# mLSTM gate rows of heads 1 to 3 spread over the partitions by a transfer through memory

## The chip, the cores and the metric

The kernel runs on one core of a Trainium2 chip. The metric is the time on the device, in microseconds, of one execution of the whole program; the median of several runs is used.

## The reference

One inference step of a two-layer decoder for a prompt of 256 tokens and eight samples of four tokens (288 token columns in all). Layer 0 has a linear recurrence and a windowed attention, layer 1 an mLSTM block, each with an MLP. The part that matters is the mLSTM of layer 1, four heads of 512 columns, each with a 512 x 512 state:

```python
m_t = jnp.maximum(log_inter, jnp.max(log_intra, axis=2))
w_intra = jnp.exp(log_intra - m_t[:, :, None, :]) * jnp.einsum('bthd,bshd->btsh', qc, kc)
w_inter = jnp.exp(log_inter - m_t)
num = jnp.einsum('btsh,bshe->bthe', w_intra, vc) + w_inter[..., None] * jnp.einsum('bthd,bhde->bthe', qc, C)
den = jnp.sum(w_intra, axis=2) + w_inter * jnp.einsum('bthd,bhd->bth', qc, n)
h = num / jnp.maximum(jnp.abs(den), jnp.exp(-m_t))[..., None]
decay = jnp.exp(bcum[:, -1] + m - m_new)
C_new = decay[..., None, None] * C + jnp.einsum('bshd,bshe->bhde', kw, vc)
```

The quantities `m_t`, `exp(-m_t)`, `w_inter` and `decay` are one number per head and token (or per head and sample). The kernel holds them as rows, one partition a head, and needs them for each head on all 128 partitions.

## The kernel before

Every engine has its own instruction stream, written out by hand; the streams meet at semaphores. Dense projections run before (`IN_C`) and after (`OUT_C`) the head stage, as float32 products in three parts (lines 2140 to 2142).

**The rows.** During the last steps of `IN_C` VectorE and ScalarE compute `rows`, 4 partitions x 616 columns: minus the running maximum (256 prompt columns), the bound of the denominator (256), then for the samples the maximum, the weight of the old state and the decay. Of these 584 (`NBC`) are to be spread. ScalarE's exponentials (lines 1060 to 1062) finish them and count `gact` up to 3; TensorE's `gate_columns` waits for that.

**The spreading.** `head_rows(h)` on TensorE (line 2546) multiplies `rows` with a selection matrix of 4 x 128 (`sel`): a product of 512 columns and one of 72 (L2548, L2549). They land in the two staging banks, 6 and 7 of the eight PSUM banks, which each staged value of a head takes in turn. The list `USES` gives the order (q0 to q3, qo, kt0, kt1, ks, vt0, vt1, vs, bc0, bc1, sc, nu0, nu1, n, mean), `staged` waits until the value two places before has been read, and `reads` works out which count of which semaphore (`stage_read_a` for ScalarE, `stage_read_v` for VectorE) that is. ScalarE's `head_rows` copies both products to `bc` in SBUF (L1134, L1135); `bc` has two buffers, taken by even and odd heads.

**The readers of `bc`.** VectorE's `queries(h)` (L1783 and behind) scales the samples' queries and counts `qs_ready`; `arguments(h)` (L1798 to L1801) writes the arguments of the exponentials and counts `ew_arg`; the denominators take a row (L1892), and each state update `new_state` (L1831) a decay column.

**The order of a head.** A head has eight rounds j = 0 to 7. In each round TensorE multiplies two blocks of the old state with the samples' queries (`old_state`, L2615) and makes two outer products (`outers`, L2654), VectorE updates the two blocks in the ring `cring` (L1831), and SyncE stores them and loads the blocks eight places ahead (L666, L657). In rounds 3 and 4 TensorE also makes the prompt's state (L2640) and ScalarE copies it out (`prompt_state`, L1168, in its rounds 2 and 3). Each engine's `chunk(h, j)` puts the work of the next head between rounds:
- round 4: q (`qk`, L2495 and L2499; ScalarE L1072, L1074); round 5: keys; round 6: values (`vt0`, `vt1`, `vs`; ScalarE L1125 to L1130, VectorE L1776)
- round 7 on TensorE: `head_rows(h + 1)`, `sum_groups` (L2624), `scores(h + 1)` (L2558, L2561)
- round 7 on ScalarE: copy of the summed old states (L1211), `head_rows(h + 1)`, group sum (L1216), its square (L1218), the three exponentials `exps(h + 1)` (L1141 to L1143, with a table load), `own_values` (`vb`, L1153), `high_rows` (L1178, which releases GpSimd L2110)
- round 7 on VectorE: `queries`, `arguments`, `weights` (L1808, L1809) of head h + 1

For head 0 the same pieces stand before the loop: on TensorE `values_by_token(0)`, `head_rows(0)`, `scores(0)`; on ScalarE `own_keys(0)`, `values_by_token(0)`, `head_rows(0)`, `exps(0)`, `own_values(0, 0)`. `own_values` writes the right-hand side of the outer products, and `outers` waits for it (`vb_ready`).

Of the kernel before, what the change touches and what calls it, by code (L numbers as in the profile page):

```python
# [19 lines left out]
F32 = mybir.dt.float32  # L20
F32R = mybir.dt.float32r
ALU = mybir.AluOpType
ACT = mybir.ActivationFunctionType
AX = mybir.AxisListType

P = 128
D = 1024
SEQ = 256
NB = 8
# [21 lines left out]
NH = 4  # L51
# [25 lines left out]
IN_AB, OUT_AB, UP0, DOWN0, IN_C, OUT_C, UP1, DOWN1 = range(8)  # L77
# [11 lines left out]
OUT0 = [sum(m // P for _, m in DENSE[:i]) for i in range(8)]  # L89
# [16 lines left out]
NBC = R_DECAY + NB  # L106
# [14 lines left out]
assert ITEMS % 2 == 0  # L121

USES = ["q0", "q1", "q2", "q3", "qo", "kt0", "kt1", "ks", "vt0", "vt1", "vs",
        "bc0", "bc1", "sc", "nu0", "nu1", "n", "mean"]
VT_BANKS = (6, 7, 2, 3, 6, 7)
AB_USES = ["qs", "q0", "ks", "k0"] + [f"{g}{m}" for m in range(MT) for g in "ri"]
DVE_READS = ("ks", "vs", "sc", "nu0", "nu1", "n")
# [24 lines left out]
def program(nc, A, O):  # L152
    ctx = ExitStack()
    with ctx:
# [119 lines left out]
        sel, o = at("sel", o, NH * P, parts=NH)  # L274
# [15 lines left out]
        rows, o = at("rows", o, NROWS, parts=NH)  # L290
# [33 lines left out]
        bc, o = at("bc", rstd_at, 2, NBC)  # L324
# [15 lines left out]
        assert AT["conv_a_w"] + T <= AT["conv_c_w"]  # L340

        ps = ctx.enter_context(nc.psum_tensor("ps", [P, 8, 512], F32))

        def qz_of1(h, e, b):
            return qz1[:, h % 2, NS * (NB * e + b):NS * (NB * e + b) + NS]
# [24 lines left out]
        def sem(name):  # L370
            sems[name] = ctx.enter_context(nc.semaphore(name))
            return sems[name]
# [19 lines left out]
        out_taken = sem("out_taken")  # L392
# [3 lines left out]
        std_ready = sem("std_ready")  # L396
        rstd_ready = sem("rstd_ready")
        x_new = sem("x_new")
        xin_hi_ready = sem("xin_hi_ready")
        xin_ready = sem("xin_ready")  # L400
        relu2_ready = sem("relu2_ready")
# [57 lines left out]
        gact = sem("gact")  # L459
        gcol_ready = sem("gcol_ready")  # L460
# [4 lines left out]
        stage_full = sem("stage_full")  # L465
        stage_read_a = sem("stage_read_a")
# [10 lines left out]
        c_new = sem("c_new")  # L477
# [43 lines left out]
        def use(h, name):  # L521

            return len(USES) * h + USES.index(name)

        def reads(u):

            by_dve = USES[u % len(USES)] in DVE_READS
            n = sum(1 for j in range(u + 1) if (USES[j % len(USES)] in DVE_READS) == by_dve)
            return (stage_read_v if by_dve else stage_read_a), n
# [184 lines left out]
        def _(act):  # L714
# [349 lines left out]
            def staged(h, name):  # L1064
                u = use(h, name)
                act.wait_ge(stage_full, u + 1)
                return ps[:, 6 + u % 2]
# [36 lines left out]
                if g == G_PARTS + 8:  # L1104
                    keys_by_token(0)


            act.wait_ge(gcol_ready, 1)
            act.activation(tokg.rearrange("p a b -> p (a b)"), ps[:, 5, 0:4 * NH], ACT.Copy)
            act.activation(tokg_s.rearrange("p a b -> p (a b)"), ps[0:NS, 5, 4 * NH:6 * NH], ACT.Copy)  # L1110
# [11 lines left out]
            def values_by_token(h):  # L1122
# [6 lines left out]
                act.activation(vtk_s, src[0:NS], ACT.Copy)  # L1129
                act.activation(vst[:, h % 2], src, ACT.Copy, scale=sel3[:, 5:6]).then_inc(vst_hi_ready, 1)  # L1130

            def head_rows(h):

                act.activation(bc[:, h % 2, 0:512], staged(h, "bc0"), ACT.Copy).then_inc(stage_read_a, 1)  # L1134
                act.activation(bc[:, h % 2, 512:NBC], staged(h, "bc1")[:, 0:NBC - 512], ACT.Copy  # L1135
                               ).then_inc(stage_read_a, 1)

            def exps(h):

# [21 lines left out]
            def prompt_state(h, half):  # L1161

                i = item(h, NB, half)
                s = i % C_SLOTS
                act.wait_ge(c_mm, i + 1)
                if i >= C_SLOTS:
                    act.wait_ge(c_out[s], 16 * (i // C_SLOTS))
                act.activation(cring[s], ps[:, banks_of(i):banks_of(i) + HD2, :], ACT.Copy).then_inc(p_new, 1)  # L1168
# [11 lines left out]
            def chunk(h, b):  # L1180
                if b == 0:
                    act.wait_ge(den_psum, h + 1)
                    act.activation(stok[:, 0, h:h + 1], ps[0:NS, 3, SEQ:SEQ + 1], ACT.Abs)
                    act.activation(dn, ps[:, 3, 0:SEQ], ACT.Abs).then_inc(den_abs, 1)
                    act.activation(z[:, ET * h:ET * h + ET], z[:, ET * h:ET * h + ET], ACT.Silu).then_inc(z_ready, 1)
                if b == 1:
                    act.wait_ge(stage_read_v, reads(use(h, "nu1"))[1])
                    act.activation(qf[:, :, 0:SEQ], hT, ACT.Square).then_inc(h_sq, 1)
                if b == 2:
                    act.activation(dn, staged(h, "mean")[:, 0:SEQ], ACT.Sqrt, bias=tiny[:, 0:1], scale=1.0 / DH  # L1190
                                   ).then_inc(stage_read_a, 1)
                    if h == 2:
                        sample_roots(0)
                if b in (2, 3):
                    if h + 1 == NH:
                        act_hi(b - 2, 0, STEP0[OUT_C])
                    prompt_state(h, b - 2)
                if b == 4 and h + 1 < NH:
                    qk(h + 1)
                if b == 5 and h + 1 < NH:  # L1200
                    keys_by_token(h + 1)
                    own_keys(h + 1)
                if b == 6 and h + 1 < NH:
                    values_by_token(h + 1)
                    if h == 2:
                        sample_high(0)
                if b == 4 and h + 1 == NH:
                    high_rows(h)
                if b == 7:
                    act.wait_ge(hs_psum, h + 1)  # L1210
                    act.activation(hs4, ps[:, 2, :], ACT.Copy).then_inc(hs_copied, 1)  # L1211
                    if h + 1 < NH:
                        head_rows(h + 1)

                    act.wait_ge(hs_sum, h + 1)
                    act.activation(hs[:, h], ps[0:NS, 3, :], ACT.Copy).then_inc(hs_taken, 1)  # L1216
                    act.wait_ge(hs_taken, h + 1)
                    act.activation(hs_junk, hs[:, h], ACT.Square, accum_out=stok[:, 1, h:h + 1]).then_inc(hs_sq, 1)  # L1218
                    if h + 1 < NH:
                        exps(h + 1)  # L1220
                        own_values(h + 1, 0)
                        high_rows(h)

            act.wait_ge(out_taken, OUT0[OUT_C])
            own_keys(0)
            values_by_token(0)
            head_rows(0)
            exps(0)
            own_values(0, 0)
            for h in range(NH):  # L1230
# [19 lines left out]
        def _(dve):  # L1250
# [527 lines left out]

            def queries(h):

                dve.wait_ge(stage_read_a, reads(use(h, "bc1"))[1])
                inter = bc[:, h % 2, R_INTER:R_INTER + NS].unsqueeze(1).to_broadcast([P, ET, NS])
                order.after(dve.tensor_tensor(qn, qo, inter, ALU.mult))  # L1783
                if h == 0:
                    dve.wait_ge(qz1_zero, 1)
                for e in range(ET):
                    most, last = qz_own(h, e)
                    order.mark(dve.tensor_copy(most, seqs(qn[:, e, 0:NS - NT])))
                    order.mark(dve.tensor_copy(last, qn[:, e, NS - NT:NS]))
                order.wait()  # L1790
                n0_t = n0_of(h).unsqueeze(2).to_broadcast([P, ET * NB, NT])
                qn_t = qn.rearrange("p e (b t) -> p (e b) t", t=NT)
                dve.tensor_tensor(qn_t, qn_t, n0_t, ALU.mult).then_inc(qs_ready, 1)
# [333 lines left out]
        def _(pe):  # L2127
# [353 lines left out]
            def staged(h, name):  # L2481

                u = use(h, name)
                if u >= 2:
                    pe.wait_ge(*reads(u - 2))
                return ps[:, 6 + u % 2]
# [56 lines left out]
                    by_token(h, f"vt{tt}", 2, lambda m: xm[:, m, PAD + P * tt:PAD + P * tt + P])  # L2543
                samples_thrice(h, "vs", 2)

            def head_rows(h):
                hsel = sel[:, P * h:P * h + P]
                pe.matmul(staged(h, "bc0"), hsel, rows[:, 0:512], start=True, stop=True).then_inc(stage_full, 1)  # L2548
                pe.matmul(staged(h, "bc1")[:, 0:NBC - 512], hsel, rows[:, 512:NBC], start=True, stop=True  # L2549
                          ).then_inc(stage_full, 1)  # L2550

            def scores(h):

# [132 lines left out]
            def chunk(h, b):  # L2686
                if b == 0:
                    denominators(h)
                    pe.matmul(ps[0:NS, 2, :], ew[0:NS, 3 * P:3 * P + NS], vtk_s, start=False, stop=False,
                              skip_group_check=True)  # L2690
                    numerators(h)
                if h == 2 and b == 1:
                    sample_turns(0)
                if h == 2 and b == 4:
                    sample_scales(0)
                if h + 1 < NH:
                    if b == 4:
                        qk(h + 1)
                    if b == 5:
                        keys_by_token(h + 1)  # L2700
                    if b == 6:
                        values_by_token(h + 1)
                    if b == 7:
                        head_rows(h + 1)
                        sum_groups(h)
                        scores(h + 1)

            pe.wait_ge(gcol_taken, 1)
            values_by_token(0)
            head_rows(0)  # L2710
            scores(0)
            for h in range(NH):
                for j in range(NB):
# [165 lines left out]
```

## Time and profile before

| | |
|---|---|
| median of 3 runs | 1102.4 us (1102.11 to 1103.18) |
| profiled execution | 1102.52 us, span 1100.7 us |
| TensorE products | busy 1050.7 us, 95% of the span |
| VectorE | busy 664.3 us, 60% |
| ScalarE | busy 530.6 us, 48% |
| GpSimd | busy 188.8 us, 17% |
| chain that ended last | TensorE 79%, VectorE 10%, ScalarE 4% |
| head stage | about 632 to 833 us |
| spread products of heads 0 to 3 | from 636.7, 682.9, 731.2 and 779.9 us |

Busy times of engines overlap; TensorE's is modelled, and its products are pipelined, so that neighbouring rows overlap. In rows of the timeline the first number is the start in us from the span's start, the second the duration in us; brackets at the end hold the idle time of that engine before the row and what ended it. `PEld` is TensorE's weight load, `SPq` and `ACTq` are DMA issues in the instruction streams of SyncE and ScalarE.

### The profile page before, as it was taken

How to read it: one execution, taken by the hardware profiler on the slowest of the kernel's cores; microseconds unless marked ns; L12 is line 12 of the kernel's file. 1: busy time of each engine (PE TensorE's matmuls, PEld its weight loads, DVE VectorE, ACT ScalarE, POOL GpSimd, SP SyncE). 2: the span in 40 equal slices, each digit the busy share in tenths (PEclk: the TensorE clock that was granted, in tenths of full speed). 3: DMA queues.
4: the chain of work that ended last, by engine and by line, in shares of the span. 5: the costliest groups of instructions: out<-in, count | busy, mean ns of one | idle time of the engine just before them, and what ended most of it. 6: DMA issues, size and time to landing. Idle time of an engine off the chain costs nothing.

```text
span 1100.7 us, 21592 instructions
## 1 busy us (share of the span) xinstructions
PE 1050.7 (95%) x8473; PEld 912.0 (83%) x8473; DVE 664.3 (60%) x975; ACT 530.6 (48%) x865; POOL 188.8 (17%) x250
## 2 busy tenths in 40 slices
PE   6999999899999999999899999899989999999995
PEld 6988787688999999999899945363529999999995
DVE  5567694643485564335997566767784485564333
ACT  6333654533566553436565344462624466553431
POOL 5134000000114230101400420412100104230100
PEclk9999999999999999999999999999989999999998
DMA  9799887999545445454743069999998435454531
GB/s 349 261 349 337 315 339 282 381 376 409 177 135 171 159 168 171 159 167 137 273 152 118 1 212 406 351 400 349 375 402 322 160 134 172 164 162 171 166 120 43
DMA packets 92762, 261.23 MB, mean 237 GB/s; under 512 B 8933, under 2 KB 10085, under 8 KB 92409
## 3 DMA queue, kind: packets, MB, share of 16 engines
q1 hardware_dynamic: 91818, 258.69, 65.5%
q0 software_dynamic: 432, 1.29, 0.4%
q8 instruction: 55, 0.90, 0.3%
q14 instruction: 25, 0.20, 0.1%
q10 hardware_dynamic: 432, 0.14, 0.1%
HBM read 218.36 MB, written 41.73 MB: 236 GB/s over the span
## 4 chain that ended last, share of the span: by engine, by line
PE 79%; DVE 10%; ACT 4%; issue 2%; DMA 2%; POOL 2%; SPq 1%; DVEq 0%; ACTq 0%
PE ps L2140 20%; PE ps L2141 20%; PE ps L2142 20%; PE ps L2252 2%; PE ps L2654 1%; DVE cring L1831 1%; PE ps L2615 1%; PE ps L2640 1%; PE ps L2507 1%; PE ps L2333 1%; DVE w_lo L1256 1%; DMA kv_a<-in_kv 1%; PE ps L2234 1%; DVE x L1350 1%; PE ps L2495 1%
## 5 line engine op out<-in xcount | busy, mean ns | idle before, releaser
L1256 DVE TENSOR_TENSOR w_lo<-w_raw,w_hi 128x1024 fp32r<-128x1024 f32 x232 | 286.5, 1241 | 211.3 <-ACT w_hi L723 210.4
L723 ACT ACTIVATE w_hi<-w_raw 128x1024 fp32r<-128x1024 f32 x232 | 242.4, 1054 | 209.0 <-PE ps L2142 166.5
L2140 PE MATMUL ps<-xin_hi,w_hi 128*128 128x288 f32 x1016 | 304.9, 300 | 13.6 <-DVE w_lo L1256 13.6
L2141 PE MATMUL ps<-xin_lo,w_hi 128*128 128x288 f32 x1016 | 301.6, 297 | 0.0
L2142 PE MATMUL ps<-xin_hi,w_lo 128*128 128x288 f32 x1016 | 301.3, 297 | 0.0
L2140 PEld LDWEIGHTS ps<-xin_hi,w_hi 128*128 128x128 f32 x1016 | 192.8, 190 | 25.5 <-DVE w_lo L1256 15.1
L2141 PEld LDWEIGHTS ps<-xin_lo,w_hi 128*128 128x128 f32 x1016 | 192.9, 190 | 0.7
L2142 PEld LDWEIGHTS ps<-xin_hi,w_lo 128*128 128x128 f32 x1016 | 192.7, 190 | 0.0
L2141 PE MATMUL ps<-hid_lo,w_hi 128*128 128x288 f32 x512 | 151.0, 295 | 0.0
L2142 PE MATMUL ps<-hid_hi,w_lo 128*128 128x288 f32 x512 | 150.9, 295 | 0.0
L2140 PE MATMUL ps<-hid_hi,w_hi 128*128 128x288 f32 x512 | 150.2, 293 | 0.0
L2140 PEld LDWEIGHTS ps<-hid_hi,w_hi 128*128 128x128 f32 x512 | 96.3, 188 | 0.0
L2141 PEld LDWEIGHTS ps<-hid_lo,w_hi 128*128 128x128 f32 x512 | 96.3, 188 | 0.0
L2142 PEld LDWEIGHTS ps<-hid_hi,w_lo 128*128 128x128 f32 x512 | 96.2, 188 | 0.0
L1831 DVE SCALAR_TENSOR_TENSOR cring<-cring,bc,ps 128x1024 f32<-128x1024 f32 x64 | 79.0, 1276 | 26.8 <-PE ps L2654 26.5
L1995 POOL TENSOR_TENSOR hid_lo<-relu,hid_hi 128x288 f32 x64 | 61.6, 965 | 160.7 <-ACT hid_hi L805 160.7
L1371 DVE SCALAR_TENSOR_TENSOR relu<-ps,rstd 128x288 f32<-128x288 f32 x64 | 29.0, 456 | 62.0 <-PE ps L2142 56.2
L803 ACT ACTIVATE relu<-relu 128x288 f32<-128x288 f32 x64 | 28.2, 441 | 63.4 <-DVE relu L1371 58.7
L1985 POOL COPY sqsum<-sq 128x288 f32<-128x288 f32 x5 | 2.9, 570 | 296.8 <-ACT sq L791 289.4
L1988 POOL TENSOR_TENSOR sqsum<-sqsum,sq 128x288 f32<-128x288 f32 x31 | 25.0, 808 | 147.9 <-ACT sq L791 146.9
L791 ACT ACTIVATE sq<-ps 128x288 f32<-128x288 f32 x32 | 13.2, 412 | 69.5 <-PE ps L2142 69.5
L2654 PEld LDWEIGHTS ps<-vb,kst 64*128 64x128 f32 x128 | 13.0, 190 | 37.4 <-issue 20.3
(421 smaller groups left out, 1665.7 us busy)
## 6 DMA issues: line engine op xcount, KB each, us to landing
w_raw<-in_weights SPq DMA_DIRECT2D x232, 512.0 KB, 3.4
cring<-in_C SPq DMA_DIRECT2D x64, 512.0 KB, 6.4
out_Cs<-cring SPq DMA_DIRECT2D x64, 512.0 KB, 7.2
kv_a<-in_kv SPq DMA_DIRECT2D x56, 448.0 KB, 6.2
kv_b<-in_kv SPq DMA_DIRECT2D x52, 448.0 KB, 6.2
kv_w<-in_kv SPq DMA_DIRECT2D x20, 448.0 KB, 7.5
out_Cp<-cring SPq DMA_DIRECT2D x8, 512.0 KB, 6.7
out_v<-gaqkv SPq DMA_DIRECT2D x1, 1152.0 KB, 15.0
```

Of the source, the lines that this page charges most:

```text
L723: act.activation(w_hi[:, l % UM], w_raw[:, l % W_SLOTS], ACT.Copy).then_inc(hi_ready, 1)
L803: act.activation(relu2[:, l % 2], relu[:, l % 2], ACT.Square).then_inc(relu2_ready, 1)
L1256: dve.tensor_tensor(w_lo[:, l % W_SLOTS], w_raw[:, l % W_SLOTS], w_hi[:, l % UM], ALU.subtract).then_inc(lo_ready, 1)
L1371: dve.scalar_tensor_tensor(relu[:, l % 2], ps[:, bank, 0:T], 0.0, rstd, ALU.max, ALU.mult).then_inc(out_taken, 1)
L1831: dve.scalar_tensor_tensor(cring[s], cring[s], bc[:, h % 2, R_DECAY + b:R_DECAY + b + 1], new, ALU.mult, ALU.add).then_inc(c_new, 1)
L1988: pool.tensor_tensor(sqsum, sqsum, sq[:, m % 2], ALU.add).then_inc(sq_added, 1)
L1995: pool.tensor_tensor(hid_lo[:, bass.ds(m, 1)].rearrange("p a t -> p (a t)"), relu2[:, l], hid_hi[:, bass.ds(m, 1)].rearrange("p a t -> p ( ...
L2140: pe.matmul(out, w_hi[:, j, ws], hi, start=start and kk == 0, stop=False)
L2141: pe.matmul(out, w_hi[:, j, ws], lo, start=False, stop=False)
L2142: last = pe.matmul(out, w_lo[:, l % W_SLOTS, ws], hi, start=False, stop=stop and kk == UK - 1)
L2252: last = pe.matmul(ps[32 * b4:32 * b4 + 32, 4 + c, 0:NK // 2], qz_of[b4][:, h], kv[s][:, c * NK // 2:(c + 1) * NK // 2], start=h == 0, sto ...
L2654: last = pe.matmul(ps[:, banks_of(i) + d, :], kst[own, h % 2, P * e:P * e + P], vb[own, (HALF_B * h + p) % 2], start=True, stop=True)
```

## The change

The rows of all heads are stored once to an array in memory (`row_copy`), by a DMA from ScalarE's queue. For heads 1 to 3 a DMA from ScalarE's queue, issued in round 3 of the head before, reads one row and writes it to all 128 partitions of `bc`. The uses `bc0` and `bc1` go out of the list, so that `sc` follows `vs`. Head 0 keeps the products, in banks 3 and 2, with one count of `gcol_ready` behind both, and ScalarE copies them as `first_rows`. The ScalarE copies add 8 each to `bc_in` and the DMAs 16; VectorE's `queries` waits for that count.

```diff
 USES = ["q0", "q1", "q2", "q3", "qo", "kt0", "kt1", "ks", "vt0", "vt1", "vs",
-        "bc0", "bc1", "sc", "nu0", "nu1", "n", "mean"]
+        "sc", "nu0", "nu1", "n", "mean"]
...
+        row_copy = nc.dram_tensor("row_copy", [NH, NBC], F32).ap()
...
@@ ScalarE
+            act.wait_ge(gact, 3)
+            act.dma_start(row_copy, rows[:, 0:NBC]).then_inc(rows_out, 16)
             act.wait_ge(gcol_ready, 1)
...
+            def first_rows():
+
+                act.wait_ge(gcol_ready, 2)
+                act.activation(bc[:, 0, 0:512], ps[:, 3, :], ACT.Copy).then_inc(bc_in, 8)
+                act.activation(bc[:, 0, 512:NBC], ps[:, 2, 0:NBC - 512], ACT.Copy).then_inc(bc_in, 8)
+
             def head_rows(h):
 
-                act.activation(bc[:, h % 2, 0:512], staged(h, "bc0"), ACT.Copy).then_inc(stage_read_a, 1)
-                act.activation(bc[:, h % 2, 512:NBC], staged(h, "bc1")[:, 0:NBC - 512], ACT.Copy
-                               ).then_inc(stage_read_a, 1)
+                act.wait_ge(rows_out, 16)
+                if h >= 2:
+                    act.wait_ge(c_new, 2 * NB * (h - 1))
+                act.dma_start(bc[:, h % 2], row_copy[h:h + 1].to_broadcast([P, NBC])).then_inc(bc_in, 16)
...
                     prompt_state(h, b - 2)
+                if b == 3 and h + 1 < NH:
+                    head_rows(h + 1)
...
                     act.activation(hs4, ps[:, 2, :], ACT.Copy).then_inc(hs_copied, 1)
-                    if h + 1 < NH:
-                        head_rows(h + 1)
-
...
             values_by_token(0)
-            head_rows(0)
+            first_rows()
             exps(0)
...
@@ VectorE, queries
-                dve.wait_ge(stage_read_a, reads(use(h, "bc1"))[1])
+                dve.wait_ge(bc_in, 16 * (h + 1))
...
@@ TensorE
-            def head_rows(h):
-                hsel = sel[:, P * h:P * h + P]
-                pe.matmul(staged(h, "bc0"), hsel, rows[:, 0:512], start=True, stop=True).then_inc(stage_full, 1)
-                pe.matmul(staged(h, "bc1")[:, 0:NBC - 512], hsel, rows[:, 512:NBC], start=True, stop=True
-                          ).then_inc(stage_full, 1)
+            def first_rows():
+
+                hsel = sel[:, 0:P]
+                pe.wait_ge(out_taken, OUT0[OUT_C])
+                pe.matmul(ps[:, 3, :], hsel, rows[:, 0:512], start=True, stop=True)
+                pe.matmul(ps[:, 2, 0:NBC - 512], hsel, rows[:, 512:NBC], start=True, stop=True).then_inc(gcol_ready, 1)
...
                     if b == 7:
-                        head_rows(h + 1)
                         sum_groups(h)
                         scores(h + 1)
...
             values_by_token(0)
-            head_rows(0)
+            first_rows()
             scores(0)
```

ScalarE from the prompt state of head 0 to the q of head 1, before (line numbers in rows of the change are its own, some 3 to 11 higher):

```order
L1168 ACTIVATE cring_164<-ps 128x1024
L1168 ACTIVATE cring_167<-ps 128x1024
L1153 ACTIVATE vb<-vst,sel_119 128x512
L1072 ACTIVATE qf<-ps 128x288 x4
L1074 ACTIVATE qo<-ps 128x128
```

And in the change:

```order
L1179 ACTIVATE cring_164<-ps 128x1024
L1179 ACTIVATE cring_167<-ps 128x1024
L1147 DMA bc<-row_copy 128x584
L1164 ACTIVATE vb<-vst,sel_119 128x512
L1075 ACTIVATE qf<-ps 128x288 x4
L1077 ACTIVATE qo<-ps 128x128
```

The load of the next head's rows stands between the second prompt state and `vb`; nothing else moved there.

ScalarE at the start of head 1 (`hs_110` is `hs4`, the summed old states), before:

```order
L1130 ACTIVATE vst<-ps,sel_119 128x512
L1211 ACTIVATE hs_110<-ps 128x512
L1134 ACTIVATE bc<-ps 128x512
L1135 ACTIVATE bc<-ps 128x72
L1216 ACTIVATE hs<-ps 32x512
L1218 ACTIVATE hs_junk,stok<-hs 32x512
L1141 ACT_TABLE_LOAD
L1141 ACTIVATE ew<-ew,tokg 128x256
```

And in the change:

```order
L1134 ACTIVATE vst<-ps,sel_119 128x512
L1224 ACTIVATE hs_110<-ps 128x512
L1226 ACTIVATE hs<-ps 32x512
L1228 ACTIVATE hs_junk,stok<-hs 32x512
L1152 ACT_TABLE_LOAD
L1152 ACTIVATE ew<-ew,tokg 128x256
```

The two copies to `bc` are gone; the rest keeps its order.

TensorE at the same place, before:

```order
L2654 MATMUL ps<-vb,kst 128x512 x4
L2548 MATMUL ps<-rows,sel 128x512
L2549 MATMUL ps<-rows,sel 128x72
L2624 MATMUL ps<-hs_110,four_eyes 32x512
L2558 MATMUL ps<-qf,xcc 128x256 x4
L2558 MATMUL ps<-qf,xcc 128x128 x4
L2561 MATMUL ps<-qf,xcc 32x32 x4
```

And in the change:

```order
L2665 MATMUL ps<-vb,kst 128x512 x4
L2635 MATMUL ps<-hs_110,four_eyes 32x512
L2569 MATMUL ps<-qf,xcc 128x256 x4
L2569 MATMUL ps<-qf,xcc 128x128 x4
L2572 MATMUL ps<-qf,xcc 32x32 x4
```

The group sum and the scores now follow the outer products directly.

## Rows read from the trace of the kernel before

**Rows 1.** The page, the chain that ended last, share of the span

```profile
PE 79%; DVE 10%; ACT 4%; issue 2%; DMA 2%; POOL 2%; SPq 1%; DVEq 0%; ACTq 0%
```

**Rows 2.** Timeline at the start of head 1

```profile
682.26 0.73 PE L2654 MATMUL ps<-vb,kst 64*128 64x512 f32 x4
682.61 0.57 ACT L1211 ACTIVATE hs<-ps 128x512 f32<-128x512 f32 x1
...
683.34 2.46 DVE L1831 SCALAR_TENSOR_TENSOR cring<-cring,bc,ps 128x1024 f32<-128x1024 f32 x2
...
684.15 1.04 PE L2624 MATMUL ps<-hs,four_eyes 128*32 128x512 f32 x2
...
685.13 2.69 PEld L2558 LDWEIGHTS ps<-qf,xcc 128*128 128x128 f32 x16 [0.84 <-ACT bc L1135]
...
686.59 1.28 ACT L1141 ACT_TABLE_LOAD   x1
...
687.55 0.17 DVE L1801 TENSOR_TENSOR ew<-bc,stri 32x32 f32<-32x32 f32 x1
687.89 0.51 ACT L1141 ACTIVATE ew<-ew,tokg 128x256 f32<-128x256 f32 x1
...
688.81 0.70 ACT L1153 ACTIVATE vb<-vst,sel 128x512 fp32r<-128x512 f32 x1
...
689.58 0.33 PEld L2654 LDWEIGHTS ps<-vb,kst 64*128 64x128 f32 x4 [1.25 <-DVE ew L1809]
```

**Rows 3.** Timeline at the starts of heads 2 and 3

```profile
735.78 0.17 DVE L1801 TENSOR_TENSOR ew<-bc,stri 32x32 f32<-32x32 f32 x1
736.12 0.51 ACT L1141 ACTIVATE ew<-ew,tokg 128x256 f32<-128x256 f32 x1
...
785.12 0.51 ACT L1141 ACTIVATE ew<-ew,tokg 128x256 f32<-128x256 f32 x1 [0.22 <-DVE ew L1801]
```

**Rows 4.** Timeline at the start of head 0

```profile
637.05 0.66 ACT L1130 ACTIVATE vst<-ps,sel 128x512 fp32r<-128x512 f32 x1
...
638.49 0.44 PE L2549 MATMUL ps<-rows,sel 4*128 4x72 f32 x2 [0.63 <-DVE vst L1776]
...
638.96 0.23 ACT L1135 ACTIVATE bc<-ps 128x72 f32<-128x72 f32 x1 [0.47 <-PE ps L2549]
639.23 0.29 DVE L1783 TENSOR_TENSOR qn<-qo,bc 128x128 f32<-128x128 f32 x1 [0.79 <-ACT bc L1135]
```

**Rows 5.** Timeline of ScalarE: a DMA issue, before head 0, behind head 0's prompt state

```profile
1.69 0.45 ACTq L825 DMA_DIRECT2D ident<-in_ident  x1
...
632.72 0.69 ACT L1119 ACTIVATE kst<-ps,w 128x512 fp32r<-128x512 f32 x1 [3.52 <-issue]
...
667.46 0.71 ACT L1153 ACTIVATE vb<-vst,sel 128x512 fp32r<-128x512 f32 x1
...
669.07 0.90 ACT L1072 ACTIVATE qf<-ps 128x288 f32<-128x288 f32 x2 [0.89 <-PE ps L2495]
```

**Rows 6.** State transfers: issue (min/median/max ns), landing, one load, its block's use

```profile
L666 SPq DMA_DIRECT2D out_Cs<-cring x64: 372/508/1462, 645.1 to 827.4; - x64
...
DMA to landing us min/median/max: 3.1/6.5/11.2
...
668.80 0.38 SPq L657 DMA_DIRECT2D cring<-in_C  x1
...
681.29 1.04 PE L2615 MATMUL ps<-cring,qz 128*32 128x512 f32 x8
```

**Rows 7.** Windows of TensorE: us, busy (instructions), granted clock, DMA share, GB/s

```profile
683.00:690.00 7.00, 6.63 (x42) 1.00 1.05 405
697.00:704.00 7.00, 5.40 (x29) 1.00 0.92 270
...
812.00:819.00 7.00, 4.62 (x24) 0.99 1.05 408
819.00:826.00 7.00, 6.55 (x17) 0.52 1.05 408
```

More of the change, by code:

```diff
@@ L398, in program @@
         x_new = sem("x_new")
+        rows_out = sem("rows_out")
+        bc_in = sem("bc_in")
         xin_hi_ready = sem("xin_hi_ready")
```

## Prediction

> **What bounds the kernel now.** I read the page first, then the chain of waits, then the order of time around each place where the gate rows are spread. The chain that ended last is 79% TensorE [rows 1], so work taken from another engine counts only where TensorE waits for it, and work taken from TensorE counts only where TensorE waits for nothing else. The change touches only the mLSTM head stage, about 632 to 833 us, so I read that stage at its four head starts.
>
> Head 1 is the pattern [rows 2]. TensorE ends the last outer products of head 0 (682.26 + 0.73 = 682.99), makes the two spread products (not shown), then the group sum L2624 at 684.15, and starts the scores L2558 only at 685.13, having waited 0.84 us for ScalarE's copy of the rows. That looks like a loss on the bounding engine. But TensorE stops again at 689.58, with 1.25 us of idle weight load, before the first outer products of head 1. The profile names VectorE's L1809; the value that L2654 needs by the code is `vb`, made by ScalarE L1153 from 688.81 to 689.51. That copy stands behind the three exponentials. The exponentials wait for two things: the table load (686.59 + 1.28 = 687.87) and VectorE's arguments (L1801, ended 687.55 + 0.17 = 687.72). VectorE began them behind two state updates that ran until 683.34 + 2.46 = 685.80. So the head start is set by VectorE's updates and arguments, with ScalarE's table load 0.15 us behind them, and the spread products lie beside it.
>
> **The change, part by part.** Everything is summed against the profiled execution of 1102.52 us (span 1100.7 and 1.8 around it), which is 0.12 us above the median of the three runs, 1102.40.
>
> *Heads 1 and 2.* Two products leave TensorE and two copies leave ScalarE. The group sum can start when ScalarE's `hs4` copy is done (682.61 + 0.57 = 683.18), so near 683.25 and not 684.15, and the scores right behind it near 684.3 and not 685.13: 0.8 to 0.9 us earlier. They end that much earlier, and TensorE then waits longer at L2654; I cost this at nothing, and what hides it is VectorE's chain up to 687.72. If that cover were gone, 0.85 us a head would come through. ScalarE's group-sum copy, square and table load move up by the same 0.9 us, so the load ends near 687.0. Then the exponentials wait for the arguments alone: 687.72 plus the 0.04 us that lie between a copy's end and the start of what it releases in head 0 (639.19 and 639.23, [rows 4]), so 687.76 and not 687.89: 0.13 us. What is late next is VectorE. Head 2 repeats it: arguments end 735.95, exponential at 736.12 [rows 3], so 0.13 again. The same 0.13 passes on through ScalarE's `y_hi` to GpSimd, which the chain runs through afterwards. Together 0.26 us; bounds 0 and 2 x 0.85 = 1.7.
>
> *Head 3.* The exponential already waited 0.22 us for the arguments [rows 3]. Nothing to gain: 0.
>
> *Head 0* still uses the products, but into banks 3 and 2 and not into the staging banks 6 and 7. Before, the second product started only at 638.49, when VectorE had read `vst` out of its bank; ScalarE's small copy then ended at 638.96 + 0.23 = 639.19 and VectorE's queries started at 639.23 [rows 4]. Now both products stand right behind the sample values, before 638.0 by their lengths, and ScalarE, free at 637.05 + 0.66 = 637.71, copies both from about 638.0. A 512-column and a 72-column copy end near 638.7, so the queries start near 638.73: 0.50 us. The whole head waits for these queries (arguments, exponentials, first `vb`). Bounds: 0 if ScalarE still comes late, and the 0.79 us of idle that VectorE's row shows there if the rows are ready as soon as it is free.
>
> *The DMA issues.* Four go into ScalarE's queue. At the kernel's start one costs 0.45 us there [rows 5]. The store of the rows stands before `tokg`; ScalarE idles 3.52 us a little later, before `kst` at 632.72 [rows 5], so it costs nothing. The three loads stand between the prompt state copy L1168 and `vb` L1153. In head 0, L1153 ends 668.17 and ScalarE then idles 0.89 us for TensorE's q product before L1072 at 669.07 [rows 5]. With 0.45 us more, L1153 ends near 668.7. Cost nothing, cover left 0.4 us; if the cover were gone, each microsecond of issue beyond 0.9 us would delay the q staging that TensorE waits for, three times. The longest issue that SyncE's stores show is 1462 ns [rows 6], so the bounds are 0 and 3 x 0.6 = 1.8 us; I take 0, because ScalarE's own rows are 0.45.
>
> *The transfers.* Each load writes 128 x 584 x 4 B = 299 KB. It is issued near 667.7 and first needed at 685.8: 18 us. The state transfers of 512 KB take 6.5 us in the median and 11.2 at most [rows 6], so VectorE should never wait for it. The other side is the traffic: under such load the engines move 408 GB/s in the stretch from 812 [rows 7], so a spread takes 0.73 us of all of them away from state loads and stores. The next state load was issued at 668.80 and its block is used at 681.29 [rows 6]: 12.5 us less 6.5 leaves 6.0, so 0.73 is hidden. Cost 0, bounds 0 and 2.2 us for the three.
>
> The Trainium skill (DMA: Bandwidth & Descriptors, "Issuing engines are not separate DMA queues") says that transfers issued by ScalarE interleave with SyncE's on the same 16 engines and save only sequencer time. That speaks against the change, and by it the sum would be worse by up to those 2.2 us if the state loads had no slack; the row of 681.29 says that they have.
>
> **Sum:** 0.50 + 0.26 + 0 + 0 = 0.76 us; 1102.52 - 0.76 = 1101.8 for an execution like the profiled one, 1101.6 beside the median. I say 1101.7. A measurement of this kernel can tell about 0.2% (2.2 us) from no change, so this counts as no change.
>
> **The rivals.**
> - *TensorE bounds the head start* (faster). The spread products and the wait for them come off in full: 3 x 0.85 + 0.5 = 3.1 us, so 1099.4. For it: the 0.84 us wait in rows 2 is real. Against it: the later stop at 689.58. Chance 7%.
> - *TensorE's clock* (slower; one mechanism). The granted clock is 1.00, the 2.4 GHz level, at the start of head 1 (683 to 690). From 819 to 826 it is 0.52, nearly all at 1.2 GHz, behind a stretch in which TensorE was busy 4.62 of 7 us; in the stretch 697 to 704, busy 5.40 of 7, it was full [rows 7]. The change takes some 1.5 us of work out of each start of heads 1 to 3, and the wait before L2654 grows. If the clock fell there, 7 us at 0.52 cost up to 7 x 0.48 = 3.4 us; the denominators and numerators behind it are TensorE's own. Once: 1105.1; three times: 1111.9. It decides as soon as one head start is followed by a granted clock under 1. Chance 8%. The same fall at 819 might also move or vanish, which gives up to 3.4 us back (1098.3): 4%.
> - *ScalarE's queue blocks* (a wait that takes the place of the one removed). The issue takes 1.46 us and not 0.45 under the full load of the DMA engines: 1101.8 + 1.8 = 1103.6, no change by the measure. Chance 8%.
> - *The shared engines.* The state loads behind a spread come late in full: 1101.8 + 2.2 = 1104.0. Against it: 6 us of slack. Chance 6%.
>
> The Trainium skill (TensorE: Matmul & The Clock Gate, "Part 1: The HAM clock gate") says that activity releases the throttle and idleness brings it back. By that rule taking products away from a stretch that already waits can cost more than they took; [rows 7] agree as to the fall at 819, and no row here shows it at a head start.
>
> **How the numbers follow.** Forecast 67%, faster rivals 11%, clock 8%, queue 8%, shared engines 6%. The forecast with the bounds of its terms runs from 1100 to 1102.5; to hold 8 in 10 the range takes in the queue and the shared engines above and the first faster rival below: 1099.4 to 1104.2. Faster by over 0.2% (under 1100.2): 0.12. Slower (over 1104.6): 0.09. Same: 0.79.
>
> **What would show it.** In the profile after: queries of head 0 about 0.5 us earlier behind `vst`; scores of heads 1 to 3 about 0.85 us earlier behind the last outer products, yet the next L2654-line products only 0.1 us earlier; exponentials of heads 1 and 2 released by the arguments and not by the table load; four issues of about 0.45 us on ScalarE's queue with idle time left before the q copies; no wait for `bc` from a DMA. I am wrong if a head start is more than 0.5 us shorter or longer in heads 1 to 3, if the queries wait for the load, or if the granted clock behind a head start is under 1.

## The result and the profile after

The change takes 1104.71 us in the median of 9 executions (1101.55 to 1106.71), before 1102.17 (9 executions, 1099.5 to 1103.18). The ratio is 1.0026, 95% interval 1.0015 to 1.0037: slower by some 2.9 us (the medians differ by 2.5), just above the range that was given (up to 1104.2). The profiled execution takes 1106.54 us with a span of 1104.7, that is 4.0 us more span than before's.

The page of the change: the span, busy time of TensorE's products and weight loads with share and count, and the granted clock in tenths over 40 slices of 27.6 us:

```profile
span 1104.7 us, 21569 instructions
...
PE 1052.3 (95%) x8461; PEld 913.8 (83%) x8461; DVE 665.0 (60%) x975; ACT 528.6 (48%) x859; POOL 188.8 (17%) x250
...
PEclk9999999999999999999999989999889999999998
```

The clock's row has three slices at 8 before the last one where before's page has one. TensorE has 12 records fewer (six products in two passes each), ScalarE six fewer, and yet TensorE's busy time rose from 1050.7 to 1052.3: products took longer.

The windows of the change on TensorE: stretch, its length, busy (count), granted clock, DMA share, GB/s:

```profile
636.00:643.00 7.00, 6.14 (x41) 1.00 0.30 115
643.00:650.00 7.00, 7.00 (x29) 0.60 0.71 224
...
683.00:690.00 7.00, 6.77 (x74) 1.00 1.05 407
690.00:697.00 7.00, 5.83 (x42) 1.00 1.04 366
...
785.00:792.00 7.00, 5.80 (x47) 0.94 1.05 394
792.00:799.00 7.00, 7.00 (x27) 0.57 1.00 355
...
821.00:828.00 7.00, 6.79 (x24) 0.56 1.05 408
```

In this execution the clock is at the lower level, 1.2 GHz, behind the start of head 0 and again behind the start of head 3, where before shows none; the fall at the end of head 3 was there before too [rows 7]. The starts of heads 1 and 2 keep the full clock. Before, behind the starts of heads 0 and 3:

```profile
643.00:650.00 7.00, 6.95 (x46) 1.00 0.55 155
...
786.00:793.00 7.00, 6.42 (x44) 1.00 0.96 335
```

The timeline at head 0, answering to [rows 4]:

```profile
636.49 0.66 ACT L1134 ACTIVATE vst<-ps,sel 128x512 fp32r<-128x512 f32 x1
...
637.25 0.60 ACT L1139 ACTIVATE bc<-ps 128x512 f32<-128x512 f32 x1
...
638.00 0.53 DVE L1793 TENSOR_TENSOR qn<-qo,bc 128x128 f32<-128x128 f32 x1
...
642.06 0.74 PE L2665 MATMUL ps<-vb,kst 64*128 64x512 f32 x4 [0.86 <-DVE ew L1819]
...
645.62 1.22 PE L2598 MATMUL ps<-ew,vtk 128*128 128x256 f32 x2
...
652.09 0.74 PE L2665 MATMUL ps<-vb,kst 64*128 64x512 f32 x4
```

The same places of head 0 before:

```profile
643.05 0.74 PE L2654 MATMUL ps<-vb,kst 64*128 64x512 f32 x4
...
646.03 0.70 PE L2587 MATMUL ps<-ew,vtk 128*128 128x256 f32 x2
...
649.84 0.73 PE L2654 MATMUL ps<-vb,kst 64*128 64x512 f32 x4
```

The stage starts 0.56 us earlier in this execution (`kst` at 632.16, before 632.72), so times are read from there. The queries come 5.84 us behind `kst` and not 6.51: 0.67 us gained. The first outer products come 9.90 us behind it and not 10.33 (`kst` 632.72, L2654 at 643.05): 0.43 gained, 0.24 less than at the queries, whose first instruction now takes 0.53 us and not 0.29. But from the first outer products to the second (round 1) it is 652.09 - 642.06 = 10.03 us, in before 649.84 - 643.05 = 6.79: 3.24 us lost while the clock is down. A numerator pair of 256 columns takes 1.06 to 1.22 us and not 0.60 to 0.70. No product left TensorE at head 0, so this fall does not stand behind missing work. What changed there is where TensorE waits: before 0.25 us in front of the first spread product and 0.63 in front of the second [rows 4], now not there, but 0.86 us in one piece in front of the outer products.

At head 1, answering to [rows 2], all engines:

```profile
684.51 0.73 PE L2665 MATMUL ps<-vb,kst 64*128 64x512 f32 x4
684.86 0.57 ACT L1224 ACTIVATE hs<-ps 128x512 f32<-128x512 f32 x1
...
685.48 1.04 PE L2635 MATMUL ps<-hs,four_eyes 128*32 128x512 f32 x2 [0.23 <-ACT hs L1224]
685.55 0.38 SPq L660 DMA_DIRECT2D cring<-in_C  x1
685.59 2.46 DVE L1841 SCALAR_TENSOR_TENSOR cring<-cring,bc,ps 128x1024 f32<-128x1024 f32 x2
...
686.46 2.88 PE L2569 MATMUL ps<-qf,xcc 128*128 128x256 f32 x16
...
687.92 1.28 ACT L1152 ACT_TABLE_LOAD   x1
...
689.80 0.17 DVE L1811 TENSOR_TENSOR ew<-bc,stri 32x32 f32<-32x32 f32 x1
690.01 0.51 ACT L1152 ACTIVATE ew<-ew,tokg 128x256 f32<-128x256 f32 x1 [0.81 <-DVE ew L1811]
...
691.74 0.73 PE L2665 MATMUL ps<-vb,kst 64*128 64x512 f32 x4 [1.17 <-DVE ew L1819]
```

The scores start 1.22 us behind the end of the outer products (686.46 against 685.24) where it was 2.14 (685.13 against 682.99). The exponential is released by VectorE's arguments and no longer by the table load. From outer products to outer products it is 7.23 us (684.51 to 691.74), before 7.35 (682.26 to 689.61): 0.12 gained. TensorE's products wait 1.17 us at the end of it, before 0.37:

```profile
689.61 0.73 PE L2654 MATMUL ps<-vb,kst 64*128 64x512 f32 x4 [0.37 <-DVE ew L1809]
```

Over all four heads the waits at this place are 4.4 us in the change and were 1.3 before.

At head 3 the same stretch as in head 0, from the first to the second outer products, is 10.03 us (788.86 to 798.89), before 6.79 (786.84 to 793.63): 3.24 lost, all under the lower clock.

The transfers, by the line of their issue (ns min/median/max on ScalarE's queue) and their landing:

```profile
L1147 ACTq DMA_DIRECT2D bc<-row_copy x3: 326/327/356, 668.8 to 765.1; - x3
...
DMA to landing us min/median/max: 5.5/6.6/7.0
```

No row of the waits names them, and no VectorE wait for `bc` is there. The issue at 668.80 runs beside the copy of 1.02 us that starts at 668.79, and ScalarE still idles 0.89 us before the q copies, as before.

The differences add up to those of the spans (change less before): -0.56 us ahead of the stage; -0.43 up to the first outer products of head 0; +3.24 in head 0; -0.23 from there to the first outer products of head 3 (788.86 - 642.06 less the 3.24 is 143.56, before 786.84 - 643.05 = 143.79); +3.24 in head 3; -1.27 from its second outer products to the last sample gate (835.46 - 798.89 = 36.57, before 831.47 - 793.63 = 37.84). That is +3.99, and the spans differ by 4.0. The last term is no gain of the change: the fall at the end of head 3 is in both executions. It fits a part of head 3's loss coming back, since TensorE's waits for VectorE's state updates before outer products went from 2.7 us over the stage to 1.7.

### The profile page after: what moved, and what is told of

It reads as the page before. It is cut to its first block, busy times and chain, and to the rows that moved or that the text cites. A ratio compares the mean times of both kernels' runs of the same rounds, so it can differ in the third digit from the quotient of the medians.

```text
span 1104.7 us, 21569 instructions
## 1 busy us (share of the span) xinstructions
PE 1052.3 (95%) x8461; PEld 913.8 (83%) x8461; DVE 665.0 (60%) x975; ACT 528.6 (48%) x859; POOL 188.8 (17%) x250
## 4 chain that ended last, share of the span: by engine, by line
PE 80%; DVE 10%; ACT 4%; POOL 2%; DMA 2%; issue 2%; SPq 0%; DVEq 0%; ACTq 0%
PE ps L2150 20%; PE ps L2151 20%; PE ps L2152 20%; PE ps L2262 2%; DVE cring L1841 2%; PE ps L2665 2%; PE ps L2626 1%; PE ps L2651 1%; PE ps L2517 1%; PE ps L2343 1%; DVE w_lo L1266 1%; PE ps L2244 1%; DMA kv_a<-in_kv 1%; PE ps L2214 1%; PE ps L2505 1%
```

## The experiments

Three accounts of the loss were open. *Clock*: TensorE falls to 1.2 GHz behind head starts, because work was taken out of a stretch that already waits. *Transfers*: the issues and the traffic cost what was taken for hidden. *Head 0*: its new order, not heads 1 to 3. Each kernel ran in 12 executions (one in 11), beside 29 or 35 of before. Single executions differ by some us, also in where the head stage starts (630.1 to 633.1 us over all the profiled ones), so the ratios decide, and with them the granted clock as the mean over all executions of a kernel. For before that is 0.9909 in the first set of runs, 0.9904 in the second; for the change 0.9852 in its first nine.

**Head 0's part alone.** The change's `first_rows` on TensorE and ScalarE, the product and copy helpers of before for heads 1 to 3:

```diff
-            head_rows(0)
+            first_rows()
...
+                if h == 0:
+                    dve.wait_ge(bc_in, 16)
+                else:
+                    dve.wait_ge(stage_read_a, reads(use(h, "bc1"))[1])
```

> Only head 0 of the change: its spread products go to banks 3 and 2 right behind the sample values; heads 1 to 3 keep products and copies as before, no transfer. Clock theory (the time went into stretches of TensorE at 1.2 GHz behind the starts of heads 0 and 3): the queries start some 0.6 us earlier, and if the fall behind head 0 comes from this part, the granted clock from 643 to 650 is about 0.6 and the time about 3 us over its gain, so +2.0 to +2.8 us against before; if it does not, -0.5 to -1.0 us. Transfer theory (the time went into the DMA issues and the traffic): -0.6 us and a full clock at every head start.

1101.78 us against 1101.88, ratio 1.0000 (0.9987 to 1.0013), mean clock 0.9902. Its queries come 5.83 us behind `kst` (637.74 against 631.91), so the 0.67 us are there, and the stage from 643 to 650 keeps its clock in the profile. The part neither makes the loss nor shows its gain within the interval. One of its twelve executions has a clock of 0.986 and takes 1105.69 us, beyond all 35 of before (0.988 and 1104.5 at most), so a costly fall may come with this part too, but rarely.

**Heads 1 to 3 alone.** The transfers for heads 1 to 3, head 0 through the staging banks as before:

```diff
+                act.activation(bc[:, 0, 0:512], staged(0, "bc0"), ACT.Copy).then_inc(stage_read_a, 1)
...
-                dve.wait_ge(bc_in, 16 * (h + 1))
+                if h == 0:
+                    dve.wait_ge(stage_read_a, reads(use(0, "bc1"))[1])
+                else:
+                    dve.wait_ge(bc_in, 16 * h)
```

> Only heads 1 to 3 of the change: their rows come by transfer; head 0 keeps its products in the staging banks. Clock theory: head 0 at full clock as before, a fall behind at least one of heads 1 to 3 (head 3 in the profile of the change), so +2 to +3.5 us for each fall, less 0.3. Transfer theory: the same +2 to +4 us, but with a full clock and longer waits on ScalarE's queue or for the state loads.

1104.14 us against 1101.88, ratio 1.0028 (1.0016 to 1.0039), mean clock 0.9872. This part alone gives the whole loss. Its profiled execution happened to be the shortest of the twelve (1102.53 us, clock 0.993), with one short fall that starts in the stretch from 697 to 704 (0.88 there); the fall is a matter of the single execution, which the mean clock shows better than one profile.

**The transfers alone.** Before, with the store and the loads added into columns that nobody reads:

```diff
+                if b == 3 and h + 1 < NH:
+                    act.wait_ge(rows_out, 16)
+                    act.wait_ge(bc_in, 32 * h)
+                    for i, dst in enumerate(scratch):
+                        src = row_copy[h + 1:h + 2, HN * i:HN * i + HN]
+                        act.dma_start(dst, src.to_broadcast([P, HN])).then_inc(bc_in, 16)
```

> Before, with all products and copies kept, plus the store of the rows and, in round 3 of heads 0 to 2, loads of the same 299 KB from ScalarE's queue (in two halves of 292 columns, into parameter columns that nobody reads any more, since SBUF has no free place of the whole size; so twice the issues). Clock theory: within 0.5 us of before. Transfer theory: +2 us or more, as the change itself.

1102.47 us against 1101.88, ratio 1.0003 (0.9991 to 1.0015), mean clock 0.9930: nothing that can be told from zero, with twice the load issues. ScalarE's timeline behind the prompt state of head 0:

```profile
664.10 1.02 ACT L1174 ACTIVATE cring<-ps 128x1024 f32<-128x1024 f32 x1 [5.45 <-PE ps L2653]
664.16 0.91 ACTq L1209 DMA_DIRECT2D par<-row_copy  x2
665.18 0.72 ACT L1159 ACTIVATE vb<-vst,sel 128x512 fp32r<-128x512 f32 x1
666.62 0.90 ACT L1077 ACTIVATE qf<-ps 128x288 f32<-128x288 f32 x2 [0.72 <-PE ps L2508]
```

Both issues (0.91 us) lie inside the copy of 1.02 us that ScalarE had just started, so even they take nothing from the idle time behind. The transfers are not the loss: at most 1.7 us (1.0015) could be theirs, and the next run has them without any loss.

**The products kept, unused.** The change, and in round 7 of heads 0 to 2 its two products back on TensorE, into bank 3; the outputs do not depend on them:

```diff
+            def same_products(h):
...
+                pe.wait_ge(den_abs, h + 1)
+                hsel = sel[:, P * h:P * h + P]
+                pe.matmul(ps[:, 3, :], hsel, rows[:, 0:512], start=True, stop=True)
+                pe.matmul(ps[:, 3, 0:NBC - 512], hsel, rows[:, 512:NBC], start=True, stop=True)
```

> The change, with the two products of 512 and 72 columns put back on TensorE at their old place in heads 1 to 3, into bank 3, where nobody reads them; no copy. Clock theory: a full clock behind the starts of heads 1 to 3, the fall behind head 0 stays if head 0's part makes it, so 3 us less than the change. If the clock does not depend on these products, the same time as the change (+2.5 us against before).

1101.18 us against 1101.88, ratio 0.9995 (0.9986 to 1.0003), mean clock 0.9926. TensorE at the start of head 1:

```profile
680.84 1.12 PE L2643 MATMUL ps<-rows,sel 4*128 4x512 f32 x2
681.80 0.33 PE L2644 MATMUL ps<-rows,sel 4*128 4x72 f32 x2
682.07 1.04 PE L2635 MATMUL ps<-hs,four_eyes 128*32 128x512 f32 x2
```

With the same transfers, the same copies gone and the same order of everything else, 1.23 us of TensorE's work that nobody reads (680.84 to 682.07), at each of three places, takes the loss away: 1101.18 us where heads 1 to 3 alone took 1104.14 beside it, with the mean clock up from 0.9872 to 0.9926. That is the clock account's sharpest forecast. Head 0's new order is in this kernel too. In its profiled execution TensorE waits 0.37 us again before the first outer products of head 1, and the clock is full behind the starts of all four heads; it still falls from about 700 to 706 and at the end of head 3 (0.989 over all).

**The change again**, in one set with the next three.

> The change itself again, beside the three others. Every theory: 1.002 to 1.004 of before. Clock theory: the granted clock of its executions is lower than before's on average (about 0.985 against 0.991), and the executions with the higher clock are the shorter ones.

1103.26 us against 1101.79, ratio 1.0015 (1.0003 to 1.0026), mean clock 0.9870. The loss is there again, smaller; the two intervals of the change overlap from 1.0015 to 1.0026. Its four executions at a clock of 0.989 or 0.990 take 1100.43, 1100.81, 1101.31 and 1102.73 us, the two at 0.985 and below 1105.35 and 1105.81. Its profiled execution is of the same program as the one above and 6.1 us shorter (1100.43 against 1106.54). The windows show where its clock was low:

```profile
643.00:650.00 7.00, 7.00 (x42) 1.00 0.75 234
685.00:692.00 7.00, 5.83 (x30) 0.78 1.03 386
692.00:699.00 7.00, 7.00 (x34) 0.73 0.59 228
762.00:769.00 7.00, 6.56 (x28) 0.76 1.05 407
...
792.00:799.00 7.00, 7.00 (x40) 1.00 0.98 345
```

Now it is head 1 and a place in head 2, and heads 0 and 3 are at full clock behind their starts. TensorE at head 1:

```profile
686.39 0.74 PE L2665 MATMUL ps<-vb,kst 64*128 64x512 f32 x4 [1.17 <-DVE ew L1819]
...
696.43 0.74 PE L2665 MATMUL ps<-vb,kst 64*128 64x512 f32 x4
...
700.20 0.70 PE L2673 MATMUL ps<-qf,ones 128*128 128x256 f32 x2
700.83 0.74 PE L2665 MATMUL ps<-vb,kst 64*128 64x512 f32 x4
```

And in the profiled execution above, where head 1 was at full clock:

```profile
703.96 0.70 PE L2673 MATMUL ps<-qf,ones 128*128 128x256 f32 x2 [1.61 <-POOL qf L2115]
```

The first round takes 10.04 us (686.39 to 696.43), as behind heads 0 and 3. But the second takes only 4.40 (696.43 to 700.83), before 6.06 (696.40 to 702.46): the wait of 1.6 us for GpSimd at the squares (L2673) is gone, because TensorE comes later. So half of this fall is paid out of a wait that was there anyway, and from the first to the third outer products it costs 1.6 us (14.44 against 12.85). Behind heads 0 and 3 no such wait follows in the next round, and the whole 3.24 us stay up to the third outer products (14.42 against 11.18). Its stage, from `kst` to the last sample gate, is 199.3 us (630.07 to 829.38), in the other execution of the change 203.3 (632.16 to 835.46), before 198.75 (632.72 to 831.47). 2.1 us of the 6.1 lie ahead of the stage and have nothing to do with the change; 4.0 lie in it.

**The wait filled instead.** The change, with unused products of 288 columns where TensorE waits before the first outer products (1, 2, 2, 2 for heads 0 to 3):

```diff
+                    if j == 0:
+                        banks_free(item(h, 0, 0))
+                        busy_products(ps[:, banks_of(item(h, 0, 0))], (1, 2, 2, 2)[h])
```

> The change, with products of 288 columns that nobody reads (bank 0 or 4, before the outer products overwrite it) in TensorE's wait before the first outer products: one for head 0, two for heads 1 to 3 (0.6 us each, the wait is 0.9 and 1.2 us). Clock theory: the wait is filled and the head starts lose no work, so no fall behind them; 2 to 3.5 us less than the change, that is -1 to +0.5 us against before. If it was not the missing work but something else in the change (transfers, the shared engines), the same time as the change or up to 0.4 us more.

1101.53 us against 1101.79, ratio 0.9999 (0.9988 to 1.0010), mean clock 0.9914. TensorE at the start of head 1, with the filling in the row L2646:

```profile
687.21 1.02 PE L2626 MATMUL ps<-cring,qz 128*32 128x512 f32 x5
688.16 1.24 PE L2646 MATMUL ps<-xcc,ident 128*128 128x288 f32 x4
689.40 0.74 PE L2670 MATMUL ps<-vb,kst 64*128 64x512 f32 x4
```

The wait of 1.17 us is gone from its record, and from outer products to outer products it is 7.23 us as in the change (682.17 to 689.40). Work of another kind, in the same wait, points the same way as the old products did. By itself this run is weaker: its interval and that of the change beside it meet between 1.0003 and 1.0010.

**The end of head 3 filled, in before.** The same kind of products in rounds 5 to 7 of head 3 (3, 2, 2, into bank 6):

```diff
+                    if h + 1 == NH and j in {5: 3, 6: 2, 7: 2}:
+                        busy_products(ps[:, 6], {5: 3, 6: 2, 7: 2}[j])
```

> Before, with the same kind of unused products in TensorE's waits in rounds 5 to 7 of head 3 (three, two, two, into bank 6, free by then). Before falls to 1.2 GHz there in its profile (819 to 826, clock 0.52). Clock theory: this fall goes, and 1 to 3 us with it. Rival (the stretch is bound by the state transfers, so the clock costs nothing there): within 0.5 us of before.

1101.16 us against 1101.79, ratio 0.9998 (0.9987 to 1.0008), although the mean clock rises from 0.9904 to 0.9952. The rival holds here: the fall at this place costs nothing that can be told (up to 1.4 us by the interval). The next run shows a wait that bears on it.

**Everything filled.** The change, with both fillings and three products before the squares of heads 1 and 2.

> The change with both fillings, and three unused products before the squares of heads 1 and 2, where TensorE waits for GpSimd (697 to 704). Clock theory: no fall in the head stage at all, the gain of the change's own steps (0.8 us) shows, and 1 to 3 us of the end of head 3: 1098 to 1100.5 us, -1.5 to -4 us against before. Rival: the products lie in the way and cost what they take, +1 us or more over the change.

1100.45 us against 1101.79, ratio 0.9994 (0.9978 to 1.0009), mean clock 0.9958. In its profiled execution no fall is left in the head stage, and still only a part of the forecast gain can be seen, within the interval. The timeline of the last round of head 3:

```profile
812.44 0.38 SPq L660 DMA_DIRECT2D cring<-in_C  x1
...
817.81 1.05 PE L2626 MATMUL ps<-cring,qz 128*32 128x512 f32 x4
...
819.62 1.05 PE L2626 MATMUL ps<-cring,qz 128*32 128x512 f32 x4 [0.76 <-DMA cring<-in_C]
```

At full clock TensorE comes to the last state block before it has landed (issued 812.44, used 819.62) and waits. In before it got there later, at the low clock, and the weight load of this block waited 0.24 us:

```profile
821.04 0.19 PEld L2615 LDWEIGHTS ps<-cring,qz 128*32 128x32 f32 x4 [0.24 <-DMA cring<-in_C]
```

So the last block's transfer bounds the end of the stage here, and a faster TensorE there gains a wait.

**Two more versions and a control.** The products kept plus the fillings before the squares and at the end; the change with the fillings at the starts and the end; before with the fillings before the squares and at the end.

> The change with its two products per head kept on TensorE (as in the run with the products kept) and unused products before the squares of heads 1 and 2 and in rounds 5 to 7 of head 3. Clock theory: granted clock 0.996, 1099.5 to 1101 us, the change's own gain of 0.8 us and the end of head 3 together, -1 to -2.5 us against before. Rival: the products cost what they take, at or above before.

> The change with the fillings at the head starts and in rounds 5 to 7 of head 3, none before the squares. Clock theory: as the run with all filled if the waits before the squares rarely bring a fall: clock 0.995 to 0.996, -1 to -2.5 us against before; if they often do, clock 0.992 and 0 to 1 us slower than that run.

> Before with the fillings before the squares and at the end of head 3, to tell the fillings' gain from the change's own. Clock theory: clock 0.996, -0.5 to -1.5 us against before, and 0.8 us above the two filled versions of the change, since their queries of head 0 and exponentials of heads 1 and 2 start earlier. Rival (the change's own steps gain nothing): the same time as those two.

Against 1101.37 us of before: 1100.95 (ratio 0.9999, 0.9987 to 1.0011), 1100.35 (0.9991, 0.9980 to 1.0001) and 1101.92 (1.0007, 0.9995 to 1.0019). The second has the lowest ratio of all versions tried, 1 us under before by its median, but its interval takes in 1; none is shown to beat before. The control comes out above the second by 1.6 us in the median, which speaks for a gain of the change's own steps, but their intervals overlap and their fillings are not at the same places, so that gain is measured only in the trace (0.43 us at head 0's outer products, 0.1 each at heads 1 and 2), not in the time.

## Why the prediction was wrong

- **What failed** is the sentence in the part on heads 1 and 2, "I cost this at nothing, and what hides it is VectorE's chain": the longer wait of TensorE was priced only by what is on the path. The cover was real, the outer products moved by 0.12 us as forecast, but the wait had a second price, the clock of the products behind it. The step that should have carried it stood among the rivals, "TensorE's clock", with its place and a price of up to 3.4 us a fall, and a chance of 8%. A fall behind the start of head 0 or 3 cost 3.24 us (10.03 against 6.79), one behind head 1 net 1.6.
- **Why the chance was too low.** It was set by whether the fall comes or not, from one profiled execution of before. In the change it comes at some of the four places, and not at the same ones in the two profiled executions: the mean clock is 0.985 over nine executions of the change, 0.991 over 35 of before. Spread over all, the loss is a little more than the dearest fall's cost: 2.9 us plus the 0.7 gained (0.43 + 0.23). The range ended at 1104.2, 0.5 under the result, since it left this rival out.
- **The sum's own terms held.** Head 0: 0.67 us at the queries and 0.43 at the first outer products, said 0.50. Heads 1 and 2: 0.12 at head 1 (said 0.13), released by the arguments. Head 3: 788.86 - 739.85 = 49.01 us from head 2's outer products, before 786.84 - 737.84 = 49.00: nothing, as said.
- **Transfers.** Issue 0.33 us (said 0.45), landing 6.6 us (said 6.5 from the 512 KB ones), no wait; alone they cost nothing that can be told (1.0003). The cover of ScalarE's idle time was not even needed, since the issue ran beside the copy.
- **A wait that was none.** The prediction has TensorE waiting 0.84 us for the copy of the rows before the scores at 685.13, and takes that as what speaks for the fastest rival. The 0.84 us are idle time of the weight load; the products were busy with the group sum from 684.15 to 685.19. In the change, with no such copy, the weight load at the same place is idle 0.84 us again. In the same way the 1.25 us at 689.58 are the weight load's; the products waited 0.37. The sum rests on neither, but the wait that the change would lengthen was smaller, and the group sum and the scores had followed the spread products without a gap.
- **TensorE bounds the head start**: fell, by the wait of 1.17 us at 691.74. **ScalarE's queue** and **the shared engines**: fell with the runs of the transfers alone (at most 1.7 us by its interval) and of the products kept.
- **The Trainium skill.** The section "Issuing engines are not separate DMA queues" (the Trainium skill, DMA: Bandwidth & Descriptors) says that transfers started by different engines interleave on the same 16 engines. Here the first load fell into a stretch at 403 GB/s (668 to 676), and alone the transfers cost nothing that can be told. That the slack of the state loads hid them is the prediction's reading; no run here takes the slack away. The section "Part 1: The HAM clock gate" (the Trainium skill, TensorE: Matmul & The Clock Gate) says that activity releases the throttle; it was to be weighed heavier. The runs agree: the mean clock is 0.9926 with the products kept and 0.9914 with the wait filled, against 0.9852 to 0.9872 in the kernels with neither.
- What remains argued: that the lower clock is due to the wait being longer and not to some property of the six products. Two different fillings at two places raise the clock again, which leaves little room; the exact condition of a fall is not known from these runs. The fall behind head 0 in the profiled execution stays open: no product was taken out ahead of it, and head 0's part alone, with the wait in one piece too (0.84 us), shows no loss (1.0000) and a mean clock of 0.9902 against 0.9909.

## What to carry to other kernels

Work that TensorE does while it would wait anyway is not free to remove: in a stretch that already has waits, taking some 1.2 us out at three places cost 2.9 us in all, and products that nobody reads, at the old place, gave it back; others in the waits did so less clearly. Before such an edit, look at the granted clock of every execution at hand, not of one profile, and price the stretch behind the wait at half speed; where it is under full in some of them, try later work or unused products in the wait. And look at what follows a fall: a later wait for another engine pays for a part of it (1.6 of 3.25 us behind head 1), and where TensorE waits for a transfer, filling the fall gained nothing that could be told.

## What was not expected

- The same program shows the fall at different places in different executions: behind heads 0 and 3 in one, behind head 1 and in head 2 in the other. The busy share of the stretch ahead does not tell it: before was busy 6.08 of 7 us from 636 to 643 and kept its clock, the change 6.14 and lost it.
- A DMA issue on ScalarE's queue runs beside the activation in front of it (two issues, 0.91 us, inside 1.02; one of 0.36 beside a copy of 1.02). At the kernel's start, with nothing in front, an issue takes 0.42 to 0.46 us and the next follows it.
- A read of one 2.3 KB row by 128 partitions lands in 5.5 to 7.0 us under 403 GB/s, like a state transfer of 512 KB (6.5 before).
